# A first block's output projection computed as three products of rounded parts and rests

## What is computed

```python
mix = jnp.concatenate([rms_norm(o_sb, g_grp_sb[i]), rms_norm(o_mla, g_grp_mla[i])], axis=-1) @ w_o[i]
x = x + rms_norm(mix, g_post_mix[i])
h = rms_norm(x, g_pre_ffn[i])
u = causal_depthwise_conv(h @ w_up[i], conv_w[i], conv_b[i])
```

## Time and profile before

| | |
|---|---|
| three runs | 1019.1, 1011.3 and 1019.41 us, median 1019.1 |
| the profiled execution | 1017.39 us |
| its span, first to last instruction | 1015.5 us |
| granted clock of TensorE, mean | 0.924 |
| PE busy | 830.2 us, 82% of the span |
| DVE busy | 307.5 us |
| ACT busy | 290.9 us |
| POOL busy | 128.1 us |
| read from HBM | 296.03 MB |

### The profile page before, as it was taken

One profiled execution on the slowest core, in us unless ns is written; L12 is line 12 of the kernel. 1 busy time (PEld: TensorE's weight loads), 2 busy tenths in 40 slices (PEclk: granted clock), 3 DMA queues, 4 the chain that ended last, 5 costly groups with the idle time before them and its releaser, 6 DMA issues.

```text
span 1015.5 us, 12096 instructions
## 1 busy us (share of the span) xinstructions
PE 830.2 (82%) x5080; PEld 519.6 (51%) x5080; DVE 307.5 (30%) x662; ACT 290.9 (29%) x582; POOL 128.1 (13%) x142
## 2 busy tenths in 40 slices
PE   7998789899998999999978899667766565666664
PEld 5856435899997875477856644222312121122213
DVE  3206432566676442239742201100000010000001
ACT  2316332566665443436453210000100000000002
POOL 0011011144544110017310000000000000000000
PEclk9998989899999999999989999897888888988869
DMA  9931964264443556464535699999999999999995
GB/s 360 425 103 66 392 270 150 81 252 182 166 166 115 174 218 257 140 234 158 186 146 234 239 395 393 430 428 427 429 425 430 426 430 425 429 427 428 428 428 240
DMA packets 23677, 297.93 MB, mean 293 GB/s; under 512 B 2752, under 2 KB 3008, under 8 KB 5440
## 3 DMA queue, kind: packets, MB, share of 16 engines
q1 hardware_dynamic: 23616, 297.09, 72.2%
HBM read 296.03 MB, written 1.05 MB: 293 GB/s over the span
## 4 chain that ended last, share of the span: by engine, by line
PE 58%; DMA 31%; DVE 5%; ACT 4%; POOL 2%; issue 1%; SPq 0%; DVEq 0%; POOLq 0%
PE ps L186 57%; DMA ring<-in_exps 30%; POOL ar L217 1%; DVE ar L206 1%; ACT yT L200 1%; ACT ar L200 1%; ACT ar L197 1%; DMA ring<-in_win 1%; DVE yT L214 0%; DVE misc L596 0%; DVE yT L206 0%; ACT sq L200 0%; PE ps L619 0%; DVE yT L210 0%; DVE misc L595 0%
## 5 line engine op out<-in xcount | busy, mean ns | idle before, releaser
L186 PE MATMUL ps<-ring,sq 128*32 128x512 f32 x976 | 145.1, 733 | 72.9 <-DMA ring<-in_exps 72.6
L186 PE MATMUL ps<-ring,ar 128*32 128x512 f32 (+3 forms) x792 | 103.2, 609 | 48.8 <-DMA ring<-in_exps 39.9
L186 PEld LDWEIGHTS ps<-ring,sq 128*32 128x32 f32 x976 | 30.4, 122 | 176.1 <-DMA ring<-in_exps 118.5
L186 PE MATMUL ps<-fr 128*128 128x256 f32 (+1 forms) x660 | 102.1, 311 | 3.4 <-DVE fr L206 3.4
L186 PE MATMUL ps<-hT,ring 128*128 128x256 f32 (+2 forms) x416 | 93.9, 387 | 6.9 <-DMA ring<-in_win 6.9
L186 PEld LDWEIGHTS ps<-fr 128*128 128x128 f32 x660 | 92.3, 197 | 9.6 <-DVE fr L206 2.4
L186 PEld LDWEIGHTS ps<-hT,ring 128*128 128x128 f32 (+2 forms) x416 | 78.5, 190 | 20.9 <-DMA ring<-in_win 6.9
L206 DVE TENSOR_TENSOR ar<-ar,ps 128x512 f32<-128x512 f32 x9 | 6.2, 688 | 258.6 <-PE ps L186 258.6
L186 PEld LDWEIGHTS ps<-ring,ar 128*32 128x32 f32 (+1 forms) x792 | 27.2, 118 | 109.0 <-DMA ring<-in_exps 64.8
L186 PE MATMUL ps<-ar 128*128 128x512 f32 (+9 forms) x320 | 70.0, 459 | 15.9 <-DVE ar L206 8.9
L197 ACT ACTIVATE ar<-ps 128x512 f32<-128x512 f32 (+5 forms) x49 | 27.7, 568 | 164.8 <-PE ps L1534 138.9
(11 more groups left out here) (191 smaller groups left out, 952.8 us busy)
## 6 DMA issues: line engine op xcount, KB each, us to landing
ring<-in_exps SPq DMA_DIRECT2D x90, 2048.0 KB, 30.8
ring<-in_modw SPq DMA_DIRECT2D x12, 2048.0 KB, 8.4
ring<-in_wup SPq DMA_DIRECT2D x11, 2048.0 KB, 8.4
ring<-in_win SPq DMA_DIRECT2D x5, 2048.0 KB, 11.3
ring<-in_wdown SPq DMA_DIRECT2D x5, 2048.0 KB, 8.2
ar<-in_exps SPq DMA_DIRECT2D x3, 2048.0 KB, 13.1
ring<-in_wo SPq DMA_DIRECT2D x2, 2048.0 KB, 10.0
ring<-in_wgate SPq DMA_DIRECT2D x2, 2048.0 KB, 8.4
```

Of the source, the lines that this page charges most:

```text
L186: return pe(lambda e: e.matmul(o, l, r, start=start, stop=stop, skip_group_check=True), *waits, inc=inc)
```

## The change

`wo_part` now issues three products for each (j, n, k) in place of one: rounded x times rounded w, rest of x times rounded w, rounded x times rest of w, all of fp32r tiles, 128x128 stationary by 128x512 moving. For that the eight tiles of `hT` and the sixteen 128x512 pieces of `w_o` are each split: ACT copies the rounded value, then DVE or POOL subtracts it from the source. `out_low` does it for a tile of x (into `fr` 0 to 4095), `out_parts` for a piece of w (into one of eight places, each free again when PE has done with its last user).

Where they are issued: tiles 0 to 3 of x and pieces (n=0, k=0 to 3) in gap 6 of the softmax heads, together with the two `stream("wo")` calls; pieces (1, 0 to 3) right before the projection; tiles 4 to 7 of x each behind its scaling by DVE; pieces (0, 4 to 7) behind the products of (1,0), and pieces (1, 4 to 7) behind those of (1,1). A slot of `w_o` is free when its eight pieces are split, no longer when the products are done. `split` moves up in the file and is otherwise the same.

```diff
--- before.py
+++ after.py
@@ -643,7 +643,10 @@
                 mm(ps[:, b + par, 0:128], ar[0:96, q:q + 128], ar[0:96, k:k + 128], True, True,
                    t_qm, t_km, t_kmr, read[b], read[b + 1])
                 t = mm(ps[:, b + par, 128:384], ar[0:96, q + 128:q + 256], ar[0:96, k:k + 256], True, True, inc=1)
+            t_mla[0] = t
             return t
+
+        t_mla = [None]
 
         def mla_mask(i, b, s, t, t_free):
             t = v_tt(as2(s), two(b), wide(cm, 2), ALU.add, t, t_free, t_cm)
@@ -657,6 +660,23 @@
             r = rb[:, 0, :]
             t_r = wide_factor(5, [(tile(ar, k), t_osb[k // 2]) for k in range(4)], 0, 512, r)
             tg.extend(apply_norm(hT, hT, lambda k: col("g_grp", k), 4, r, t_r))
+
+        OX, OW = (0, 2048), [4096, 5120] + [7680 + 1024 * k for k in range(6)]
+        o_n, o_free, wo, th, w_o = [0], [None] * 8, {}, [None] * 8, []
+
+        def split(src, hi, lo, low, *waits):
+            t = a_copy(hi, src, *waits)
+            return low(lo, src, hi.bitcast(F32), ALU.subtract, t)
+
+        def out_low(k, t, low, *waits):
+            hi, lo = (tile(fr, k, o) for o in OX)
+            th[k] = split(tile(hT, k), hi, lo, low, t, t_osb, *waits)
+
+        def out_parts(n, k, low, *waits):
+            i = o_n[0] % 8
+            o_n[0] += 1
+            h, l = fr[:, OW[i]:OW[i] + 512], fr[:, OW[i] + 512:OW[i] + 1024]
+            wo[n, k] = i, h, l, split(w_o[n].ap(512 * k, 512), h, l, low, w_o[n].ready, o_free[i], *waits)
 
         def mla_fill(i):
             if i == 0:
@@ -669,6 +689,11 @@
                 sb_group()
             else:
                 mod_slot(i)
+            if i == 6:
+                w_o.extend([stream("wo", j) for j in range(2)])
+                for k in range(4):
+                    out_low(k, tg[k], v_tt, t_mla[0])
+                    out_parts(0, k, v_tt if k % 2 else p_tt, t_mla[0])
 
         t_om = []
         for j, t in enumerate(softmax_heads(mla_scores, mla_mask, 96 ** -0.5, vm, t_vm,
@@ -750,15 +775,20 @@
         def x_square(i, tx_):
             return a_fn(sq[:, i * 512:(i + 1) * 512], xT[:, i * 512:(i + 1) * 512], ACT.Square, tx_[2 * i + 1])
 
-        w_o = [stream("wo", j) for j in range(2)]
-
         def wo_part(j, n, ks):
             for k in ks:
-                o = k * S + 128 * j
-                t = mm(bank(2 * j + n), hT[:, o:o + 128], w_o[n].ap(k * 512, 512), k == 0, k == 7, w_o[n].ready, tg[k],
-                       read[2 * j + n], inc=int(k == ks[-1]))
+                i, wh, wl, t_w = wo[n, k]
+                xh, xl = (fr[:, o + S * k + 128 * j:o + S * k + 128 * j + 128] for o in OX)
+                o = bank(2 * j + n)
+                mm(o, xh, wh, k == 0, False, t_w, th[k], read[2 * j + n])
+                mm(o, xl, wh, False, False)
+                t = o_free[i] = mm(o, xh, wl, False, k == 7, inc=1)
             return t
 
+        for k in range(2):
+            out_parts(1, k, v_tt, t_mla[0])
+        for k in range(2, 4):
+            out_parts(1, k, v_tt, t_om)
         for n in range(2):
             for j in range(2):
                 wo_part(j, n, range(4))
@@ -767,11 +797,11 @@
                     t_r = wide_factor(5, [(tile(sq, k), t_om[k // 2]) for k in range(4)], 1, 512, r)
                     for k in range(4, 8):
                         tg.append(v_stt(tile(hT, k), tile(hT, k), col("g_grp", k), r, ALU.mult, ALU.mult, t_r, t_om))
+                        out_low(k, tg[k], v_tt)
+            for k in range(4, 8):
+                out_parts(n, k, p_tt if n and k % 2 else v_tt)
+            w_o[n].free([wo[n, k][3] for k in range(8)])
         XH, XL, FH, FL, WP = 0, 2048, 4096, 9728, 15360
-
-        def split(src, hi, lo, low, *waits):
-            t = a_copy(hi, src, *waits)
-            return low(lo, src, hi.bitcast(F32), ALU.subtract, t)
 
         wp_n, wp_free, t_oT = [0], [None] * 4, []
 
@@ -790,7 +820,6 @@
             for j in range(2):
                 t = wo_part(j, n, range(4, 8))
                 leave(j, n, 2 * j + n, t, t_sq, t_mt, t_dg)
-            w_o[n].free(t)
         t_oT.append(t)
         ahead += [weight_parts(w_up.ap(512 * k, 512), p_tt, w_up.ready) for k in range(2, 4)]
         TB = (6, 7, 0, 1)
```

## The result

| | before | changed |
|---|---|---|
| median of 20 runs each | 1013.34 us | 1007.37 us |
| lowest to highest | 1011.11 to 1020.42 | 1005.81 to 1017.48 |
| the profiled execution's span | 1015.5 us | 1004.7 us |
| mean granted clock | 0.924 | 0.930 |
| PE instructions, busy | 5080, 830.2 us | 5112, 818.2 us |

The ratio is 0.9946, with a 95% interval of 0.9926 to 0.9965: 5.5 us of 1013.3 faster, between 3.5 and 7.5. Two later comparisons of the same two kernels gave 0.9962 (0.9933 to 0.9991) and 0.9947 (0.9914 to 0.9979). That is a gain within 1%, as forecast, and somewhat more than the 3.6 us of the sum.

A forecast was written before the change was run, and what follows sets the result against it. PE was taken to bound the projection and bytes the last 430 us, with PE's savings carried to the end. Products -5.7, waits +0.7, +0.4, +0.2, +0.8 gave -3.6 us: 1013.8 from 1017.4, range 1007.7 to 1020.4.

The forecast's parts named there:

- The bound and the carry: Last 430 us set by bytes, transfers chained to PE: time PE saves at 142 to 172 us reaches the end one for one.
- Rival (c): Byte-bound part starts at the same time, so the gain does not reach the end: 1017.4 us; chance 0.05.
- The products: Projection on PE: 32 float32 products (27.5 us) replaced by 96 fp32r ones (21.8 us), 5.7 us less.
- Rival (e): Projection's fp32r products as slow as a float32 record, 41.2 us for 27.5: 1031.1 us before any wait; chance 0.01.
- The first piece: Start of the projection: PE, free at 142.57, waits 0.7 us for POOL's rest of the first w piece at 143.3.
- The third piece: First products of (0,0): POOL's rest lands at 144.6 to 145.3, PE wants it at 144.7; 0.4 us charged.
- The norm: Between the two groups of products: ACT's copies delay the sums' copy, PE's pause grows from 1.9 to 2.1 us, 0.2 more.
- Tiles 4 to 7 and the fifth piece: Behind the norm: four trips of 1.4 us, then the first piece of (0, 4 to 7) at 157.5; PE waits 0.8 us.
- The sum: Whole projection: -5.7 + 0.7 + 0.4 + 0.2 + 0.8 = -3.6 us, from 1017.4 to 1013.8 us.
- Rival (b): Projection: the parts starve PE, with DVE's and POOL's subtractions at their upper prices, some 3.1 us: 1016.9 us; chance 0.13.
- Rival (a): Projection: parts ahead of PE everywhere, so the gain comes nearly whole: 1011.7 us; chance 0.12.
- Rival (d): TensorE's clock falls behind the norm's pause and the wait at 156.7: 1017.1 us, or 1020.4 with two spells; chance 0.04.

The follow-up runs named there:

- e6: Changed kernel with all eight rests of gap 6 on DVE, none on POOL; ratio to before 0.9979, stage 26.14 us.
- e10: e9 with every rest of the projection and of the first two w_up pieces on DVE, none on POOL; ratio to before 0.9970, stage 25.57 us.
- e3: Changed kernel with the first half of the parts made behind the softmax heads instead of in gap 6; ratio to before 0.9997, stage 30.72 us.
- e4: Changed kernel computing only the rounded-by-rounded product of the three, all parts still made; ratio to before 0.9984, stage 23.97 us.
- e8: Kernel before with the k = 1 products left out, 4 of 32 float32 products, no parts made; ratio to before 0.9959, stage 26.72 us.
- e9: Changed kernel, gap 6 rests on DVE, (1,3) behind the sums' copy, rounded (0,4 to 7) between trips, their rests after; ratio to before 0.9980, stage 26.42 us.

## Why the prediction was right, point by point

**The bound and the carry** were right: between the second profiles the distance of 4.77 us at the stage's end is 4.77 at the first store of the output. Rival (c) falls, for executions whose clock elsewhere is alike.

**The products.** 27.5 to 21.8 us held: 96 records, 36 of them from 145.56 on and 48 in 11.02 us. Rival (e) falls.

**The first piece**, forecast 0.7 us: the values end about 139.44 (138.63 plus the 0.81 that they took before, 141.76 to 142.57) and the first product starts at 139.93, 0.5.

**The third piece**, forecast 0.4: this is the term that was mis-sized. Six products from 139.93 end at 139.93 + 6 x 0.227 = 141.29, the seventh starts at 142.33, so it is 1.0 us. I had put it down to POOL's slower subtraction. What ended the wait was DVE: its rest of x tile 1 took 1.30 us beside POOL and that of tile 2 1.50, to 142.18. The sum took DVE's lone price, and for the upper end I allowed 0.3 us a subtraction; it was 0.88 and 1.08. The upper end itself was misread: I took it from the 1.03 of the earlier trace rows, but the trace of before has longer ones beside POOL, of the same shape.

```profile
205.57 1.37 DVE L206 TENSOR_TENSOR fr_h<-ring,fr_h 128x512 fp32r<-128x512 f32 x1 [0.83 <-ACT fr_h L197]
...
208.86 1.48 DVE L206 TENSOR_TENSOR fr<-ring,fr 128x512 fp32r<-128x512 f32 x1 [0.22 <-ACT fr L197]
```

**The norm**, forecast 0.2: nothing. The products of (0,0) ended later, at 142.33 + 1.36 = 143.69, so ACT was done with its four copies (144.22) before the sums. The pause is 145.56 - 143.69 = 1.9 us, as before. The two errors are one: e6, where the third piece comes in time, has the norm's delay, 0.91 for 0.50.

**Tiles 4 to 7 and the fifth piece**, forecast 0.8: 36 products from 145.56 end at 153.73, the next starts at 154.39, 0.7 us. The four trips took 1.3 us each (148.24 to 153.54), for 1.4.

**The sum**: -5.7 + 0.5 + 1.0 + 0.0 + 0.7 = -3.5 against a measured -3.37 in the stage and a forecast -3.6. The absolute time came out lower than forecast, 1007.37 for 1013.8 and 0.3 us below the range's low end of 1007.7. Most of that is the base: the sum was made on an execution of 1017.4 us, and the median of 20 runs of before is 1013.34. Taken on that, the forecast would have been 1009.7. The rest is a gain larger than the sum's: 5.97 us between the medians for 3.6. The low end was the lowest of three runs less 3.6 us, so it left no room for that.

**Rival (b)**, the parts starve PE: its mechanism costs PE time at the third piece alone, 0.6 us more than I took. The two engines hindered each other more than the upper prices say, but elsewhere under cover: DVE's rest at 156.77 took 1.68 us beside POOL and PE had not come to it. **Rival (a)**: e10 shows how far it can go, 4.58 us in the stage by another order and no POOL. **Rival (d)** did not come in the change; e3 shows it behind a wait of 3.56 us and e4 behind waits of at most 1.00 us, so the short waits that I set against it were no safe ground.

**What stays open.** The ratio 0.9946 means 5.5 us, its interval ends at 3.5, and the stage explains 3.4. The changed kernel had full clock at the start of the up projection in three profiles of three, before in one of three, and each such case is worth 2.3 + 1.6 = 3.9 us. Two in three of that would be 2.6 us and would close the gap, but three profiles each don't show such a share. They are no fair sample either: those of the changed kernel are of executions of 1006.37, 1008.3 and 1009.2 us, while 17 of its 44 timed runs took 1012.51 us or more and none of these was profiled; those of before are of 1017.39, 1013.27 and 1018.7 us. And the changed kernel's profiles start the stage 2.0 us earlier on average, where nothing of the change has run on PE. The lowest runs of the two kernels lie 5.3, 3.75 and 3.18 us apart in the three comparisons, in two of them near the stage's 3.4. Further, e8, with a stage of the same length, had the slow products in its one profile. e4, with a stage 6.2 us shorter than before, was timed at 0.9984, and e6, e9 and e10 with shorter stages than the change at 0.9970 to 0.9980. So the clock in other stages weighs as much as the stage itself in these times. What decides where the half clock falls was not found, and that it comes with the instructions of the change is neither shown nor excluded.

## What to carry to other kernels

A product in three fp32r passes beats one in float32 (0.68 against 0.86 us per 128x128x512 here) only as far as its parts are made under other work: here the products gave 5.7 us and the waits for the parts took 2.2 back, and with the first parts made one step later the waits and the lower clock took more than all of it. Before a second engine is given half of such subtractions, look at what both take side by side, over all the rows where they overlap and not in one. And a change of a few microseconds is better measured as the length of its own stage, in two profiles, than by the kernel's time.

## What the runs showed of the hardware

A DVE subtraction of 128x256 took 0.42 us alone and 1.30 and 1.50 beside a POOL subtraction, longer by more than twice its own length; one of 128x512 took 0.69 alone and 1.77 to 1.79 beside POOL in e9. Those that began while POOL was at it ended just behind POOL's end: at 140.15 and 142.18 for POOL's 139.88 and 141.90 in the changed kernel, at 157.38, 159.07 and 160.78 for 156.83, 158.53 and 160.23 in e9. One that had begun before POOL kept its own length (0.68), and POOL's took longer. So the two look as if they took turns rather than shared; e10, with POOL empty, has ten in 6.10 us. I had expected half again at most, from 0.69 and 1.03. The Trainium skill, "GPSIMD Engine Reference", section Specifications, names contention between GpSimd and a DVE instruction with two SBUF inputs; the trace agrees, and shows that here both lose: POOL's 1.28 became 1.66.

The same instructions at the same place of the same kernel ran at 0.50 in one execution and at 1.00 in another (5.26 and 2.93 us for 24 products), with the same idle time before them (1.57 us). And the half clock was there, 0.51 over 6.9 us, in a stretch of e4 ahead of which no single wait for parts was longer than 1.00 us.
